# Recurrence moved behind weight remainders, and the next norm's rows from the unnormed sum, in a two-block kernel on one core

## What is computed

```python
def rg_lru(x, w_a, b_a, w_x, b_x, lam, positions):      # gated linear recurrence, 8 blocks of 128 features
    r = sigmoid(einsum("bshi,hij->bshj", xh, w_a) + b_a)
    i = sigmoid(einsum("bshi,hij->bshj", xh, w_x) + b_x)
    log_a = -LRU_C * r * softplus(-lam)
    reset = (positions == 0)[..., None]
    a = where(reset, 0.0, exp(log_a))
    mult = where(reset, 1.0, sqrt(-expm1(2.0 * log_a)))
    bx = mult * i * xf
    return scan(h = a * h_before + bx)

# end of block 1 (x: the residual stream; y_rnn uses rg_lru, y_attn an attention)
    merged = sigmoid(g_r + bg_r) * y_rnn + sigmoid(g_a + bg_a) * y_attn
    x = x + gate[:, None, :] * (merged @ w_o[l])
return rms_norm(x, g_final)

# start of block 2, layer 0
h = x
h = h + 0.5 * rmsnorm(swiglu(rmsnorm(h, g[0]), ffn1_w_in[i], ffn1_w_out[i]), g[1])
```

## Time and profile before

| | us |
|---|---|
| three runs | 1464.23, 1459.42, 1461.87 |
| their median | 1461.87 |
| profiled execution | 1465.33 |
| its span (first to last instruction) | 1462.6 |
| TensorE busy | 1426.6 (98%) |
| VectorE, ScalarE, GpSimd busy | 870.2, 717.7, 79.2 |
| mean granted TensorE clock, of full speed | 0.993 |

### The profile page before, as it was taken

One profiled execution on the slowest core, in us unless ns is written; L12 is line 12 of the kernel. 1 busy time (PEld: TensorE's weight loads), 2 busy tenths in 40 slices (PEclk: granted clock), 3 DMA queues, 4 the chain that ended last, 5 costly groups with the idle time before them and its releaser, 6 DMA issues.

```text
span 1462.6 us, 17117 instructions
## 1 busy us (share of the span) xinstructions
PE 1426.6 (98%) x6598; PEld 1175.2 (80%) x6598; DVE 870.2 (59%) x810; ACT 717.7 (49%) x728; POOL 79.2 (5%) x91
## 2 busy tenths in 40 slices
PE   7999999999999999999999999999999999999998
PEld 6787887878888887878888878888888878888886
DVE  7768686684554575765554565554674545654535
ACT  5674667444453556644543454543453544453424
POOL 0000000010000100110000020000202101100001
PEclk9999999999999999999999999999999999999999
DMA  9745545465645363336454555454554543654541
GB/s 395 281 150 212 214 148 172 170 216 190 220 175 198 138 243 116 144 134 225 172 197 166 213 186 217 176 197 172 202 201 144 194 151 115 245 176 168 196 178 43
DMA packets 40380, 272.51 MB, mean 186 GB/s; under 512 B 4609, under 2 KB 5505, under 8 KB 8706
## 3 DMA queue, kind: packets, MB, share of 16 engines
q1 hardware_dynamic: 36864, 261.65, 49.4%
q10 hardware_dynamic: 3458, 10.04, 2.0%
HBM read 270.62 MB, written 1.05 MB: 186 GB/s over the span
## 4 chain that ended last, share of the span: by engine, by line
PE 87%; DVE 9%; ACT 3%; issue 1%; POOL 0%; DMA 0%; DVEq 0%; POOLq 0%; ACTq 0%
PE acc L2011 26%; PE acc L2013 26%; PE acc L2012 26%; PE turn L2064 4%; DVE wlo L1181 3%; DVE xn L1235 1%; PE turn L2213 0%; DVE feed_lo L1219 0%; PE aux L2548 0%; DVE h L1251 0%; PE aux L2139 0%; DVE mod_part L1331 0%; DVE red L1311 0%; DVE xn L1244 0%; ACT whi L418 0%
## 5 line engine op out<-in xcount | busy, mean ns | idle before, releaser
L1181 DVE TENSOR_TENSOR wlo<-raw,whi 128x2048 fp32r<-128x2048 f32 x233 | 533.1, 2298 | 272.9 <-ACT whi L418 272.8
L2011 PE MATMUL acc<-whi,feed_hi 128*128 128x512 f32 (+1 forms) x1496 | 598.2, 400 | 8.8 <-DVE wlo L1181 7.3
L2013 PE MATMUL acc<-whi,feed_lo 128*128 128x512 f32 (+1 forms) x1496 | 585.6, 391 | 0.0
L2012 PE MATMUL acc<-wlo,feed_hi 128*128 128x512 f32 (+1 forms) x1496 | 584.7, 391 | 0.0
L418 ACT ACTIVATE whi<-raw 128x2048 fp32r<-128x2048 f32 x233 | 445.6, 1917 | 259.1 <-PE acc L2013 248.4
L2011 PEld LDWEIGHTS acc<-whi,feed_hi 128*128 128x128 f32 x1496 | 283.6, 190 | 68.9 <-DVE wlo L1181 9.0
L2013 PEld LDWEIGHTS acc<-whi,feed_lo 128*128 128x128 f32 x1496 | 283.0, 189 | 60.5
L2012 PEld LDWEIGHTS acc<-wlo,feed_hi 128*128 128x128 f32 x1496 | 283.6, 190 | 56.7 <-issue 1.2
L2011 PE MATMUL acc<-whi,hid_hi 128*128 128x512 f32 x352 | 140.0, 398 | 0.0
L2013 PE MATMUL acc<-whi,hid_lo 128*128 128x512 f32 x352 | 138.9, 394 | 0.0
L2012 PE MATMUL acc<-wlo,hid_hi 128*128 128x512 f32 x352 | 138.9, 394 | 0.0
(11 more groups left out here) (325 smaller groups left out, 864.2 us busy)
## 6 DMA issues: line engine op xcount, KB each, us to landing
raw<-in_units SPq DMA_DIRECT2D x237, 1024.0 KB, 4.9
mod_raw<-in_units SPq DMA_DIRECT2D x6, 1024.0 KB, 11.2
gpost<-in_norm_g ACTq DMA_DIRECT2D x8, 512.0 KB, 4.9
gpre<-in_norm_g ACTq DMA_DIRECT2D x6, 512.0 KB, 6.1
mod_more<-in_units SPq DMA_DIRECT2D x2, 1024.0 KB, 23.5
h<-in_x SPq DMA_DIRECT2D x2, 512.0 KB, 8.5
w_ax<-in_w_ax SPq DMA_DIRECT2D x1, 1024.0 KB, 26.0
bgate<-in_b_gate SPq DMA_DIRECT2D x1, 1024.0 KB, 27.6
```

The costliest lines, as they stand in the source:

```text
L1181: dve.tensor_tensor(wlo[:, u % RING, :], raw[:, u % RING, :], whi[:, u % RING, :].bitcast(F32), ALU.subtract).then_inc(lo_ready, 1)
L2011: pe.matmul(out, xh, wh, start=first, stop=False)
L2012: pe.matmul(out, xh, wl, start=False, stop=False)
L2013: return pe.matmul(out, xl, wh, start=False, stop=last)
```

## The change

- **The recurrence's slots.** The table becomes `RECURRENCE, KEPT, MULT, SCAN = (25, 64), (25, 65), (27, 67), (28, 67)`. `recurrence` keeps its first two operations; the other two (maximum with the mask, decay times mask) are a function `kept` with slots of its own. The first half is moved as a whole from slot 23 to 25, behind the remainders of slots 24 and 25, its root from 24 to 27, its scan from 26 to 28. The second half's `kept` stands in slot 65, behind that slot's remainder, and its root in 67 instead of 65.
- **The next norm's rows.** A new VectorE step in slot 82, `block1_gains`, waits for both gain loads and writes `gate_part` = `gpre` * `gpost` (the tile had held the gate's partial sums, which have been read by then). In `block1_sums(G_WO, t)` the rows for TensorE come directly: `xn` = (`h` * `rs`) * `gate_part`, in two halves, from the sum that isn't normed yet. After that `h` itself is scaled (`block1_h`): for tile 0 at once, for tile 1 in the FFN, behind its `feed_lo`. The `pre` calls in slots 85 and 88 are gone.
- **ScalarE.** The second sum of squares of tile 1 moves from slot 88 to behind the FFN's first `feed_hi`. That of tile 0 stays in slot 85, and waits for the scaled `h` as before.

```diff
@@ -80,7 +80,7 @@
 GATE_R, GATE_I, DECAY, GATED = (17, 57), (19, 59), (20, 63), (21, 61)
-RECURRENCE, MULT, SCAN = (23, 64), (24, 65), (26, 67)
+RECURRENCE, KEPT, MULT, SCAN = (25, 64), (25, 65), (27, 67), (28, 67)
 MOD2_SLOT, MOD2_UNITS, GATEB_SLOT = 30, (33, 34, 35, 36), 74
@@ -327,6 +327,7 @@
         rows_copied, gates_ready = sem("rows_copied"), sem("gates_ready")
+        gains_ready = sem("gains_ready")
@@ -629,9 +630,9 @@
                     hi()
-                if (s == 8 * G_WO + 5) or s == SLOTS:
+                if s == 8 * G_WO + 5:
                     after_h()
-                    pre_square(0 if s < SLOTS else 1, v1[:, 0 if s < SLOTS else 1, :])
+                    pre_square(0, v1[:, 0, :])
                 if s == 8 * G_WO:
@@ -688,6 +689,9 @@
                 feed(feed_hi, 1)
+                if not second and layer == 0:
+                    after_h()
+                    pre_square(1, v1[:, 1, :])
                 load_gains(gpost, io["norm_g"][layer, 5:6, :] if second else io["norm_g"][layer, 1:2, :],
@@ -1428,6 +1432,23 @@
+            block1_rs = []
+            def block1_gains():
+                n["pre"] += 1
+                n["post"] += 1
+                dve.wait_ge(pre_loaded, 16)
+                dve.wait_ge(post_loaded, 16)
+                dve.wait_ge(gateb_ready, 1)
+                dve.tensor_tensor(gate_part[:, :], gpre[:, :], gpost[:, :], ALU.mult).then_inc(gains_ready, 1)
+            def block1_h(t, r):
+                dve.wait_ge(normed, 2 * t + 2)
+                dve.scalar_tensor_tensor(h[:, t, :], h[:, t, :], r, gpost[:, :], ALU.mult, ALU.mult)\
+                    .then_inc(h_ready, 1)
             def block1_sums(g, t):
@@ -1463,11 +1484,14 @@
                     r = next_rstd()
+                    dve.wait_ge(gains_ready, 1)
+                    for half in halves:
+                        dve.scalar_tensor_tensor(xn[:, t, half], h[:, t, half], r, gate_part[:, half], ALU.mult, ALU.mult)\
+                            .then_inc(normed, 1)
                     if t == 0:
-                        n["post"] += 1
-                        dve.wait_ge(post_loaded, 16)
-                    dve.scalar_tensor_tensor(h[:, t, :], h[:, t, :], r, gpost[:, :], ALU.mult, ALU.mult)\
-                        .then_inc(h_ready, 1)
+                        block1_h(0, r)
+                    else:
+                        block1_rs.append(r)
                 else:
@@ -1513,6 +1537,10 @@
                 settle()
+            def kept(half):
+                t_ = xr[:, :, CONV_W - 1:]
                 dve.wait_ge(rows_copied, 1)
@@ -1593,10 +1621,8 @@
                     lo()
-                if s == 8 * G_WO + 5 or s == SLOTS:
-                    dve.wait_ge(h_ready, n["h"])
-                    for half in range(2):
-                        pre(0 if s < SLOTS else 1, half)
+                if s == 8 * G_WO + 2:
+                    block1_gains()
                 if j == 3 and s > 8:
@@ -1609,6 +1635,8 @@
                     recurrence(RECURRENCE.index(s))
+                if s in KEPT:
+                    kept(KEPT.index(s))
                 if s in SCAN:
@@ -1656,6 +1684,8 @@
                 feed(feed_lo, feed_hi, 1)
+                if not second and layer == 0:
+                    block1_h(1, block1_rs[0])
                 mul(0)
```

## The result

The changed kernel takes **1454.88 us** (median of 6 runs, 1454.35 to 1456.96); beside them on the same chip the kernel before took 1462.81 (6 runs, 1459.42 to 1465.99). The ratio is 0.9943, with a 95% interval of 0.9931 to 0.9955: faster by 7 to 10 us. The forecast was 1454.9. The profiled executions have spans of 1455.2 and 1462.6 us; TensorE's mean granted clock is 0.997 where it was 0.993.

A forecast was written before the change was run, and what follows sets the result against it. TensorE, busy in 98% of the span, was taken as the bound, so only its waits and clock count. 4.43 + 1.96 + 0.55 = 6.94 us, taken as 7.0 off the median 1461.87, gave 1454.9 us; range 1451 to 1459.

The forecast's parts named there:

- A: First half's recurrence, slot 23 to 25: TensorE's wait at slot 26 and the low clock behind it go, worth 4.43 us.
- The cover: First half, after the move: the next remainder, wanted by slot 32 at 130.2, is done by 127.1; holds by 3 us.
- The half sentence on slot 27's remainder: First half: the remainder after slot 26's would end at 114.4, ahead of slot 27.
- B: Second half, slots 64 and 65: slot 67's remainder runs behind two operations, not four; worth 1.96 us, wait of 0.7 stays.
- what is late next: Second half: VectorE's work up to the remainder pair unchanged, slot 72 just served; leak bounds 0 to 0.6, taken as 0.
- No clock comes back here: Second half, slot 67: granted clock was already 1.00 behind the old wait, so no clock gain was counted.
- C: Next norm's rows: the 1.8 us `xn` wait goes, new waits of 0.66, 1.3 and 0.5 come; worth 0.55 us.
- the rival with late loads: Slot 82: gain loads land late, VectorE waits for the gain product, and the kernel gets slower; chance 0.04.
- The clock in C: Next norm's rows: the earlier clock fall from 328.5 to 332, costing 1.3 us, was kept in the forecast.
- the rival with the holding clock: Clock holds at the next norm's rows, or a later fall goes: 1.3 to 3 us more gain, 1453; chance 0.18.
- The leak rival: Scan chain costs 0.6, SiLU's product 1.4, a second-half clock fall 1.6: gain only 3.3 us, 1458.5; chance 0.15.
- the waits only change their name: Slots 26 and 67 find the next remainder as late as the last: no gain, 1462; chance of no change 0.03.

## Why the prediction was right, step by step

**A: right.** Forecast 4.43 us, measured 4.46 (the clock's part of the forecast is 4.43 - 2.73 = 1.70, where it says 1.6; the sum doesn't use it). No wait near 113, full clock to 120. The cover held: no wait between slots 28 and 40, and the idle-free run of VectorE from 110.93 to 127.98 is the chain that was worked out. The half sentence on slot 27's remainder turned out to carry as much as the one on slot 26's: with the recurrence between the two, next to nothing of A is left.

**B: mechanism right, size wrong, 1.96 forecast and 1.07 measured.** The remainder started at 247.04, with 0.42 of idle ahead of it for ScalarE's `whi`, and slot 67 waits 0.50; the forecast's 0.7 holds the 0.2 of overlap, so the two agree. The step that failed is the one on what is late next. It says that VectorE's work up to the remainder pair is the same in amount, and looks only at that pair and slot 72. But if the work is the same in amount, then everything that stands behind it comes no earlier than before, and the first thing that stands there is `feed_lo`, for slot 68. TensorE arrives 1.9 us earlier and finds it where it was. VectorE in the kernel before:

```profile
254.57 1.28 DVE L1219 TENSOR_TENSOR feed_lo<-turn,feed_hi 128x512 fp32r<-128x512 f32 x2
```

It ends at 255.85, and slot 68 would be wanted at 252.74 + 2.75 = 255.5. To this come the 0.32 us that the forecast itself lets VectorE idle for `whi` (250.41 against 250.09): 256.2, so 0.7 late. Measured, slot 68 starts 252.91 - 249.39 = 3.52 behind slot 67 instead of 2.75, which is 0.77 lost. The bounds of the leak, 0 to 0.6, were for another slot, and the true 0.8 is outside them. The reading of slot 72 itself isn't contradicted: the 0.46 us that came up there came with remainders that started 0.54 later than in the changed kernel. In the changed kernel's own order the first of them ends 260.76 + 2.29 - 249.39 = 13.66 behind slot 67, and five slots without a wait take 5 x 2.75 = 13.75.

"No clock comes back here" was read from one execution. Of the four traces with the wait of 2.4 us, the clock fell behind it in two, for 7 and 8 matmuls (1.4 and 1.6 us); behind the 0.5 us of the split it fell in none of nine. So in the mean B gives back some clock as well, which the pair of traces above can't show.

**C: right in its waits.** Forecast 0.55, measured 0.37, of which some 0.35 is clock; the three waits were to be 0.66, 1.3 and 0.5 and are 0.59, 1.06 and 0.44. The cause given for the first two was tested by moving the square and holds. The product of the gains ran at 296.23, straight behind a remainder pair that ended at 291.83 + 4.49, so the two loads had landed within 7.6 us of the first issue at 288.60: nothing of the rival with late loads is seen. The first SiLU wasn't late: its product is at 330.82, and slot 94 behind it 7.12 us earlier than before, more than slot 91 is.

**The clock in C: wrong.** The forecast kept the fall of 1.3 us; it went, and gave 1.22. In nine traces with the new rows it never fell there, in four with the old ones always; which of the waits it hangs on wasn't separated. This was the rival with the holding clock (0.18). The rows were read too evenly: "shorter each but more of them" was no reason to keep it.

**The sum.** In the traces, 5.90 from the three places and 1.22 from the clock are 7.12, against 6.94. (The 0.35 of clock in C's first figure was in the forecast's too, which started from the same 329.20 of the earlier trace rows.) The misses of B (0.9) and of the clock (1.2, the other way) cancel nearly. The forecast's agreement with 1454.88 to 0.1 us is luck beyond that: the gain between the medians is 7.93, not 7.0, and the forecast was taken off a median of 1461.87, 0.94 under the 1462.81 of all six runs. The changed kernel run again had a median of 1456.18, and its kernel before 1462.49, a gain of 6.3.

**The leak rival** (1458.5) was right in its kind and not in its size: it had the scan chain cost 0.6, and slot 68 cost 0.8; its other two terms didn't come. That the waits only change their name is the kernel with the recurrence between the remainders: it exists one slot away from the one that was measured.

## What to carry to other kernels

When a waited-for step is moved ahead of work on its engine, everything else behind that work comes no earlier than before while the waiting engine comes earlier: list each consumer behind it in order, not only the one that was tight before. Work moved later in one engine's order takes its readers on the others along, so a consumer that isn't urgent (here a square for a norm applied much later) should be put behind the urgent ones too. Look also at what comes to stand directly ahead of a dependent operation: here a product without a neighbour between cost 0.45 us. And what a fall of the clock adds differs between executions with the same waits: compare the waits in two traces, and count the slow matmuls of each apart.

## What the hardware showed

**The same wait does and doesn't bring the clock down.** In block 1 the waits repeat to 0.05 us between executions; a wait of 2.4 us at slot 67 was followed by 0, 0, 7 and 8 matmuls at the 1.2 GHz level, and the two waits near 626 us by a fall in 6 of 13. The Trainium skill, "TensorE: Matmul & The Clock Gate", section "Part 1: The HAM clock gate", calls the activity window free-running, and the number of slow matmuls at a kernel's start variable from run to run. The thirteen traces show the like in the middle of a program, with 0 to 13 near 855 us. What I had not expected is that the fall may also be absent behind one and the same wait.

**Small GpSimd operations are held while a remainder runs on VectorE.** The same 128x1 operation on GpSimd (the first of the pair that makes a root) in the changed kernel:

```profile
304.65 0.19 POOL L1085 TENSOR_SCALAR ms<-ss 128x1 f32<-128x1 f32 x1 [283.88 <-ACT xn L439]
...
309.52 0.98 POOL L1093 TENSOR_SCALAR pre_ms<-pre_ss 128x1 f32<-128x1 f32 x1 [4.04 <-ACT v L443]
...
319.04 0.92 POOL L1085 TENSOR_SCALAR ms<-ss 128x1 f32<-128x1 f32 x1 [7.91 <-ACT xn L439]
...
327.91 0.19 POOL L1093 TENSOR_SCALAR pre_ms<-pre_ss 128x1 f32<-128x1 f32 x1 [7.32 <-ACT v L443]
```

and VectorE's remainders at those times:

```profile
308.17 2.28 DVE L1185 TENSOR_TENSOR wlo<-raw,whi 128x2048 fp32r<-128x2048 f32 x1
...
317.62 2.28 DVE L1185 TENSOR_TENSOR wlo<-raw,whi 128x2048 fp32r<-128x2048 f32 x1
...
320.62 1.41 DVE L1489 SCALAR_TENSOR_TENSOR xn<-h,rs,gate_part 128x512 f32<-128x512 f32 x2 [0.72 <-POOL rs L1086]
```

It takes 0.19 us where VectorE is idle. Where a remainder is running, it ends 0.05 to 0.06 us behind the remainder's end: 310.50 against 308.17 + 2.28, and 319.96 against 317.62 + 2.28. The Trainium skill, "SBUF — State Buffer", section "SBUF: two separate sides", says that a VectorE instruction with two SBUF inputs and a GpSimd one that reads SBUF contend for a port pair, and the one that starts first holds it for its whole instruction. The trace agrees, with 0.92 and 0.98 against 0.19; in both cases the remainder had started first. Here it bears on C: the root for tile 1 is made behind the remainder, and VectorE idles 0.72 us for it ahead of the rows, behind which stands the remainder that slot 91 waits for. That this is what the last 0.44 us of wait hang on is argued from the rows, and wasn't tried.
